# Retention products of the values as three rounded products, with split keys, weights and values, and rotation tables loaded by tile

## The chip, the core and the metric

One core of a Trainium2 chip. The metric is the device time of one execution in microseconds (us). The core has TensorE (PE in the profile; PEld is its weight load), VectorE (DVE), ScalarE (ACT), GpSimd (POOL) and SyncE (SP), which issues nearly all transfers. Each engine has its own queue and works it off in order; they wait for one another by semaphores.

## The reference

One layer of an encoder over 1024 frames of width 1024: a projection, a gated linear attention (GLA), a retention branch with rotary keys and queries, their mixture, and a convolutional feed-forward part. The change lies in the retention branch: 4 heads, key width 256, value width 512.

```python
def step(state, inp):
    qi, ki, vi = inp
    scores = jnp.einsum('bhnd,bhmd->bhnm', qi, ki) * intra_decay
    o = jnp.einsum('bhnm,bhme->bhne', scores, vi) + \
        jnp.einsum('bhnd,bhde->bhne', qi * q_decay, state)
    state = chunk_decay * state + jnp.einsum('bhmd,bhme->bhde', ki * k_decay, vi)
    return state, o
...
rq = rope(r_q.astype(f32).reshape(b, s, RET_HEADS, RET_DK), positions)
rk = rope(r_k.astype(f32).reshape(b, s, RET_HEADS, RET_DK), positions)
o_ret = retention_mixer(rq, rk, r_v.astype(f32))
o_ret = from_chunks(head_layernorm(o_ret)) * jax.nn.silu(r_g.astype(f32))
```

## The kernel before

The kernel runs in phases: normalisation, projection, GLA, retention, the output products of both branches, the mixture, the feed-forward up and down parts. Everything is written out engine by engine, with semaphore counts as the only link; nothing is scheduled automatically. Where precision is wanted, a float32 operand is split into a rounded part and a rest (`_hi`, `_lo`), and `product3` makes three products in a rounded type (fp32r) of them: hi times hi, hi times lo, lo times hi. The retention branch before makes plain float32 products.

The retention loop has RS = 32 steps e = 0 to 31, for 8 tiles of 128 frames (t = e // 4) and 4 heads (h = e % 4). "Weights times values" and "state inputs" are its two products with the values `r_v`:

- PE, step e: `key_transposes(e)` (2 transposes into KT_BANK; not in the last tile, e >= 28), `scores(e)`, for e < 28 one side piece (12 rounded products of a projection that has nothing to do with retention, L421 to L423), `out_transposes(e-2)`, `output(e-1)` (weights `r_pt` times values, and from the second tile on two products of the queries with the state), `state_inputs(e-1)` (two products of keys `r_kdt` with values; not for the last tile).
- ScalarE, step e: `keys(e)` reads KT_BANK and writes `r_kdt`, then `rstd(e-1)`, two small steps of the normalisation; in odd steps it empties a bank of the side work.
- VectorE, step e: `weights(e)` (scores times decay), `gate(e-2)`, `outputs(e-1)` (BN_STATS and BN_AGGR of PE's output, then, after `rstd`, the scaling `r_onb`), `states(e-1)`, two updates of the state. In the last tile `outputs(e-1)` comes ahead of `gate(e-2)`, and the outputs take turns in two banks (`out_bank`). In the last two steps the splitting of the next phase's operands follows (`mixed_lo`).
- GpSimd, step e: the rotation of queries and keys (two 128x512 products with `cossin`, two 128x256 sums, and the decayed queries `r_qdb`); in every fourth step it splits one slab of weights as well (`split_slab`). Its sums of step e wait for the output of step e-4. After the loop's last rotation it splits two slabs.
- SyncE, step e: loads of queries and keys four steps ahead, store of step e-2, gates, side store, values three steps ahead, and every fourth step a slab.

After the loop come `out_transposes(30)` and the first product of the next phase, `gated_half(0, 0)`, which needs the splits of ScalarE and VectorE.

## Time and profile before

| | |
|---|---|
| median of 3 runs (lowest to highest) | 2283.79 us (2283.73 to 2285.35) |
| the profiled execution, its own time | 2283.65 us |
| its span, first to last instruction | 2281.9 us |
| mean granted TensorE clock | 0.997 |
| busy: PE, DVE, ACT, POOL | 2247.3, 1209.6, 665.5, 1547.6 us |

The span is the time between the first and the last instruction of the program; the device time has 1.75 us around it. PE's busy time is the union of its records, whose ends are modelled: distances between the starts of records tell more than their lengths. A plain float32 matmul shows as two records, a rounded one as one.

### The profile page before, as it was taken

To read this page: it belongs to the slowest core of one execution; us is meant where nothing else is said; L and a number is where in the kernel's file an instruction comes from. 1 tells how busy PE (TensorE), PEld (TensorE's weight loads), DVE (VectorE), ACT (ScalarE), POOL (GpSimd) and SP (SyncE) were. 2 spreads that over 40 slices of the span, in tenths; PEclk is the share of its full clock that TensorE was granted. 3 is DMA by queue.
4 is the path that set the end of the run, shared out by engine and by line. 5 is a ranking of instruction groups with operands and counts; after the bars stand their busy time and mean duration, and the time that the engine had idled before them with its cause. 6 is when DMAs were issued, how large, how long until landed. Compare 5 with 4: busy or idle time off the path is not lost. (4 is left out here: it accounts for less than half of the span.)

```text
span 2281.9 us, 27553 instructions
## 1 busy us (share of the span) xinstructions
PE 2247.3 (98%) x10462; PEld 1834.1 (80%) x10462; DVE 1209.6 (53%) x1271; ACT 665.5 (29%) x1021; POOL 1547.6 (68%) x954
## 2 busy tenths in 40 slices
PE   8999999999999999999999999999999999999998
PEld 7888888899888888876665888878778888888887
DVE  6322222222728887844446444223867777776564
ACT  4323333221222222211113211114444444443422
POOL 5787777766446555578664468871999999964442
PEclk9999999999999999999999999999999999999999
DMA  4333333322362333265556556642222222345444
GB/s 178 102 111 111 111 111 111 111 93 100 120 232 91 106 112 117 92 209 167 161 166 210 192 207 213 225 171 107 78 74 84 84 84 83 93 158 209 144 139 152
DMA packets 174717, 309.06 MB, mean 135 GB/s; under 512 B 12225, under 2 KB 90305, under 8 KB 174593
## 3 DMA queue, kind: packets, MB, share of 16 engines
q1 hardware_dynamic: 174160, 306.27, 40.7%
q8 instruction: 81, 1.33, 0.2%
q10 hardware_dynamic: 432, 1.11, 0.1%
q14 instruction: 44, 0.35, 0.0%
HBM read 217.16 MB, written 90.18 MB: 135 GB/s over the span
## 5 line engine op out<-in xcount | busy, mean ns | idle before, releaser
L421 PE MATMUL psum<-act_hi,w_hi 128*128 128x512 f32 x1272 | 506.0, 398 | 2.6 <-POOL w_lo L3063 1.2
L423 PE MATMUL psum<-act_hi,w_lo 128*128 128x512 f32 x1272 | 497.4, 391 | 0.0
L422 PE MATMUL psum<-act_lo,w_hi 128*128 128x512 f32 x1272 | 496.4, 390 | 0.0
L421 PEld LDWEIGHTS psum<-act_hi,w_hi 128*128 128x128 f32 x1272 | 239.7, 188 | 51.1 <-POOL w_lo L3063 2.5
L423 PEld LDWEIGHTS psum<-act_hi,w_lo 128*128 128x128 f32 x1272 | 239.3, 188 | 51.6
L422 PEld LDWEIGHTS psum<-act_lo,w_hi 128*128 128x128 f32 x1272 | 239.8, 189 | 47.2
L455 POOL TENSOR_TENSOR w_hi<-w_raw,zero_col 128x1024 fp32r<-128x1024 f32 x53 | 109.2, 2060 | 167.1 <-PE psum L423 149.4
L3105 POOL TENSOR_TENSOR w_lo<-w_raw,w_hi 128x1024 fp32r<-128x1024 f32 x44 | 110.8, 2522 | 126.2 <-ACT w_hi L3116 126.2
L1530 POOL TENSOR_TENSOR k_lev<-e_t,g_x 128x896 f32<-128x896 f32 x32 | 96.3, 3011 | 127.5 <-ACT e_t L1477 92.3
L1062 POOL TENSOR_TENSOR w_lo<-w_raw,w_hi 128x512 fp32r<-128x512 f32 x80 | 105.0, 1313 | 65.0 <-ACT w_hi L1020 65.0
L2793 DVE TENSOR_TENSOR d_lob<-d_raw,d_hib 128x512 fp32r<-128x512 f32 x44 | 102.2, 2327 | 86.6 <-ACT d_hib L2787 86.6
L458 POOL TENSOR_TENSOR w_lo<-w_raw,w_hi 128x1024 fp32r<-128x1024 f32 x53 | 143.8, 2713 | 4.2
L421 PE MATMUL psum<-w_hi,act_hi 128*128 128x512 f32 (+1 forms) x384 | 139.7, 364 | 1.7 <-POOL w_lo L458 1.5
L423 PE MATMUL psum<-w_hi,act_lo 128*128 128x512 f32 (+1 forms) x384 | 139.3, 363 | 0.0
L422 PE MATMUL psum<-w_lo,act_hi 128*128 128x512 f32 (+1 forms) x384 | 139.3, 363 | 0.0
L421 PE MATMUL psum<-w_hi,d_hib 128*128 128x512 f32 x352 | 137.3, 390 | 1.4 <-DVE act_f L2832 0.7
L422 PE MATMUL psum<-w_lo,d_hib 128*128 128x512 f32 x352 | 137.0, 389 | 0.0
L423 PE MATMUL psum<-w_hi,d_lob 128*128 128x512 f32 x352 | 137.0, 389 | 0.0
L3063 POOL TENSOR_TENSOR w_lo<-w_raw,w_hi 128x512 fp32r<-128x512 f32 x80 | 125.5, 1579 | 2.8 <-ACT w_hi L3131 2.8
L421 PE MATMUL psum<-a_sums,w_hi 128*128 128x512 f32 x320 | 124.5, 389 | 0.0
L422 PE MATMUL psum<-a_sums,w_hi 128*128 128x512 f32 x320 | 124.5, 389 | 0.0
L423 PE MATMUL psum<-a_sums,w_lo 128*128 128x512 f32 x320 | 124.5, 389 | 0.0
(300 smaller groups left out, 4957.7 us busy)
## 6 DMA issues: line engine op xcount, KB each, us to landing
w_raw<-in_w_stream SPq DMA_DIRECT2D x225, 512.0 KB, 4.0
proj_scratch<-stage SPq DMA_DIRECT2D x40, 512.0 KB, 5.2
r_x<-proj_scratch SPq DMA_DIRECT2D x64, 256.0 KB, 3.2
value_scratch<-stage SPq DMA_DIRECT2D x24, 512.0 KB, 3.6
proj_scratch<-side_out SPq DMA_DIRECT2D x48, 256.0 KB, 3.0
d_raw<-ffn_scratch SPq DMA_DIRECT2D x44, 256.0 KB, 3.6
ffn_scratch<-u_lin_v SPq DMA_DIRECT2D x20, 512.0 KB, 5.8
r_v<-value_scratch SPq DMA_DIRECT2D x32, 256.0 KB, 2.7
```

The lines of the kernel that those rows point to most:

```text
L421: nc.tensor.matmul(o, s_hi, m_hi, start=start, stop=False)
L422: nc.tensor.matmul(o, s_hi, m_lo, start=False, stop=False)
L423: return nc.tensor.matmul(o, s_lo, m_hi, start=False, stop=stop)
L455: nc.gpsimd.tensor_tensor(w_hi[:, j, :], w_raw[:, j, :], zero_col[:, :].to_broadcast((P, D)), ALU.add).then_inc(sem["hi_split"], 1)
L458: nc.gpsimd.tensor_tensor(w_lo[:, j, :], w_raw[:, j, :], w_hi[:, j, :].bitcast(F32), ALU.subtract).then_inc(sem["slab_ready"], 1)
L1062: nc.gpsimd.tensor_tensor(w_lo8[:, n % 8, :], row_block(p, i), w_hi8[:, n % 8, :].bitcast(F32), ALU.subtract).then_inc(sem["u_lo"], 1)
L1530: nc.gpsimd.tensor_tensor(k_lev[:, b, :, :], levels, key.unsqueeze(1).to_broadcast((P, NL, P)), ALU.mult).then_inc(sem["g_klev"], 1)
L2793: nc.vector.tensor_tensor(d_lob[:, slot, :], d_raw[:, slot, :], d_hib[:, slot, :].bitcast(F32), ALU.subtract).then_inc(sem["d_lo"], 1)
L3063: nc.gpsimd.tensor_tensor(w_lo8[:, n % 8, :], block_raw(p, i), w_hi8[:, n % 8, :].bitcast(F32), ALU.subtract).then_inc(sem["u_lo"], 1)
L3105: nc.gpsimd.tensor_tensor(w_lo[:, j, :], w_raw[:, j, :], w_hi[:, j, :].bitcast(F32), ALU.subtract).then_inc(sem["slab_ready"], 1)
```

## The change

The values are split into `r_v_hi` (ScalarE, `values_hi`) and `r_v_lo` (VectorE, in the place of `r_v`), the keys into `r_kdt` (now a rounded type) and `r_kdt_lo`, the weights into `r_pt_hi` and `r_pt_lo`. `output` and `state_inputs` call `product3`. ScalarE makes one copy more in each step, VectorE three or four instructions, PE waits for `r_lo`. The rotation tables `cossin` are kept for two tiles instead of all eight and come with the queries of head 0. At e = 28 four loads go ahead of the slab's load instead of behind it.

```diff
-            cossin = sb(s, "cossin", (P, 2, SEQ))
+            cossin = sb(s, "cossin", (P, 2, 2, P))
+        def values_hi_count(e):
+            return RS - HEADS + e + 1 if last_tile(e) else 2 * e + 2
...
+        def rope_tables(sp, t, landed):
+            sp.dma_start(cossin[:, t % 2, :, :], rope_d[:, :, tile_cols(t)].rearrange("a p n -> p a n")
+                         ).then_inc(landed, 16)
...
+                if h == 0:
+                    rope_tables(sp, t, r_in[h])
...
-                if e % 4 == 0:
-                    stream_load(sp, SL_SIDE + 23 + e // 4)
                 if e == MIXED_STEP - 2:
                     sp.wait_ge(sem["r_rope"], 2 * RS)
                     sp.wait_ge(sem["r_qd"], RS)
-                    for h in range(HEADS):
-                        sp.wait_ge(r_v_in[h], 32 + 16 * NT)
                     for i in range(4):
+                        sp.wait_ge(r_v_in[i], 32 + 16 * NT)
                         mixed_load(sp, i)
+                if e % 4 == 0:
+                    stream_load(sp, SL_SIDE + 23 + e // 4)
...
+            def values_hi(e):
+
+                h = e % HEADS
+                act.wait_ge(r_v_in[h], 32 + 16 * (e // HEADS) + 16)
+                if e >= 2:
+                    act.wait_ge(sem["r_u"], min(e - 1, RS - HEADS))
+                    act.wait_ge(sem["r_o"], e - 1)
+                nc.scalar.activation(r_v_hi[:, e % 2, :], r_v[:, h, :], ACT.Copy
+                                     ).then_inc(sem["r_kd"], 1)
...
+                values_hi(e)
...
-                nc.vector.tensor_tensor(r_pt[:, e % 2, :], psum[:, RS_BANK, 0:P], ret_dec[:, e % HEADS, :], ALU.mult
+                raw = r_pt[:, e % 2, :]
+                nc.vector.tensor_tensor(raw, psum[:, RS_BANK, 0:P], ret_dec[:, e % HEADS, :], ALU.mult
                                         ).then_inc(sem["r_P"], 1)
+                dve.wait_ge(sem["r_P"], 3 * e + 1)
+                nc.vector.tensor_copy(r_pt_hi[:, e % 2, :], raw).then_inc(sem["r_P"], 1)
+                dve.wait_ge(sem["r_P"], 3 * e + 2)
+                nc.vector.tensor_tensor(r_pt_lo[:, e % 2, :], raw, r_pt_hi[:, e % 2, :].bitcast(F32), ALU.subtract
+                                        ).then_inc(sem["r_P"], 1)
+
+            def low_parts(e):
+
+                h, b = e % HEADS, e % 2
+                if not last_tile(e):
+                    dve.wait_ge(sem["r_kd"], 2 * e + 1)
+                    if e >= 2:
+                        dve.wait_ge(sem["r_u"], e - 1)
+                    nc.vector.scalar_tensor_tensor(r_kdt_lo[:, b, :], psum[:, KT_BANK, 0:RET_DK], ret_k[:, h:h + 1],
+                                                   r_kdt[:, b, :].bitcast(F32), ALU.mult, ALU.subtract
+                                                   ).then_inc(sem["r_lo"], 1)
+                dve.wait_ge(sem["r_kd"], values_hi_count(e))
+                nc.vector.tensor_tensor(r_v_lo[:, h, :], r_v[:, h, :], r_v_hi[:, b, :].bitcast(F32),
+                                        ALU.subtract).then_inc(sem["r_lo"], 1)
...
+                if e < RS - 1:
+                    low_parts(e)
...
                 if e == RS - 2:
                     weights(RS - 1)
+                    low_parts(RS - 1)
...
             def key_transposes(e):
                 if e:
-                    pe.wait_ge(sem["r_kd"], e)
+                    pe.wait_ge(sem["r_kd"], 2 * e - 1)
+                    pe.wait_ge(sem["r_lo"], 2 * e - 1)
...
-                pe.wait_ge(sem["r_P"], e + 1)
+                pe.wait_ge(sem["r_P"], 3 * e + 3)
+                pe.wait_ge(sem["r_kd"], values_hi_count(e))
+                pe.wait_ge(sem["r_lo"], values_hi_count(e))
...
-                last = nc.tensor.matmul(o, r_pt[:, b, :], r_v[:, h, :], start=True, stop=e < HEADS)
+                last = product3(o, r_pt_hi[:, b, :], r_pt_lo[:, b, :], r_v_hi[:, b, :], r_v_lo[:, h, :], True, e < HEADS)
...
-                pe.wait_ge(sem["r_kd"], e + 1)
+                pe.wait_ge(sem["r_kd"], 2 * e + 2)
+                pe.wait_ge(sem["r_lo"], 2 * e + 2)
...
-                    last = nc.tensor.matmul(psum[:, U_BANK + a, :], r_kdt[:, e % 2, a * P:(a + 1) * P],
-                                            r_v[:, e % HEADS, :], start=True, stop=True)
+                    cols = slice(a * P, (a + 1) * P)
+                    last = product3(psum[:, U_BANK + a, :], r_kdt[:, e % 2, cols], r_kdt_lo[:, e % 2, cols],
+                                    r_v_hi[:, e % 2, :], r_v_lo[:, e % HEADS, :], True, True)
```

The diff leaves out the places of the new tiles, the renamed semaphore of the rotation angles, and the matching counts. In `low_parts(e)` the call comes on VectorE between `outputs(e-1)` (in the last tile `gate(e-2)`) and `states(e-1)`.

VectorE in step 9 of the loop, before, from the gating on (the names in brackets are the semaphores waited for):

```order
L1995 TENSOR_TENSOR r_ogb<-psum,r_x 128x512 [waits r_ogst1,r_onT,gate_in3]
L2004 BN_STATS r_bst<-psum 128x6 [waits r_o]
L2006 BN_AGGR r_mvb<-r_bst 128x2 [waits r_bn]
L2011 TENSOR_SCALAR r_onb<-psum,r_mvb,r_rsb 128x512 [waits r_onT,r_mv,r_rstd]
L2022 SCALAR_TENSOR_TENSOR r_st<-r_st,psum 128x512 [waits r_u]
L2022 SCALAR_TENSOR_TENSOR r_st<-r_st,psum 128x512
L1986 TENSOR_TENSOR r_pt<-psum,ret_dec 128x128 [waits r_o,r_S]
```

The same place with the change:

```order
L2042 TENSOR_TENSOR r_ogb<-psum,r_x 128x512 [waits r_ogst1,r_onT,gate_in3]
L2051 BN_STATS r_bst<-psum 128x6 [waits r_o]
L2053 BN_AGGR r_mvb<-r_bst 128x2 [waits r_bn]
L2058 TENSOR_SCALAR r_onb<-psum,r_mvb,r_rsb 128x512 [waits r_onT,r_mv,r_rstd]
L2029 SCALAR_TENSOR_TENSOR r_kdt_lo<-psum,ret_k,r_kdt 128x256 [waits r_u,r_kd]
L2033 TENSOR_TENSOR r_v_lo<-r_v,r_v_hi 128x512 [waits r_kd]
L2069 SCALAR_TENSOR_TENSOR r_st<-r_st,psum 128x512 [waits r_u]
L2069 SCALAR_TENSOR_TENSOR r_st<-r_st,psum 128x512
L2014 TENSOR_TENSOR r_pt<-psum,ret_dec 128x128 [waits r_o,r_S]
L2017 CAST r_pt_hi<-r_pt 128x128 [waits r_P]
L2019 TENSOR_TENSOR r_pt_lo<-r_pt,r_pt_hi 128x128 [waits r_P]
```

The two low parts stand between the scaling `r_onb` and the state updates, and the weights of the next step are three instructions.

PE in step 9, from output 8 to the key transposes of step 10, in the kernel before, where L2089 is the product with the state, L2099 the state inputs and L2059 the key transposes (this place and the next are the same step of the loop):

```order
L2086 MATMUL psum<-r_v,r_pt 128x512 [waits r_state,rows_in0,r_on,r_qd,r_P]
L2089 MATMUL psum<-r_st,r_qdb 128x512 x2
L2099 MATMUL psum<-r_v,r_kdt 128x512 [waits r_state,r_kd]
L2099 MATMUL psum<-r_v,r_kdt 128x512
L2059 MATMUL psum<-ident,r_qk 128x128 [waits r_kd,r_rope]
L2059 MATMUL psum<-ident,r_qk 128x128
```

With the change:

```order
L428 MATMUL psum<-r_v_hi,r_pt_hi 128x512 [waits r_qd,r_state,r_lo,r_on,r_kd,r_P]
L429 MATMUL psum<-r_v_lo,r_pt_hi 128x512
L430 MATMUL psum<-r_v_hi,r_pt_lo 128x512
L2141 MATMUL psum<-r_st,r_qdb 128x512 x2
L428 MATMUL psum<-r_v_hi,r_kdt 128x512 [waits r_state,r_lo,r_kd]
L429 MATMUL psum<-r_v_lo,r_kdt 128x512
L430 MATMUL psum<-r_v_hi,r_kdt_lo 128x512
L428 MATMUL psum<-r_v_hi,r_kdt 128x512
L429 MATMUL psum<-r_v_lo,r_kdt 128x512
L430 MATMUL psum<-r_v_hi,r_kdt_lo 128x512
L2110 MATMUL psum<-ident,r_qk 128x128 [waits r_lo,r_kd,r_rope]
L2110 MATMUL psum<-ident,r_qk 128x128
```

The transposes of the keys (L2110) now wait for `r_lo` too, and both products with the values are rows of L428 to L430.

VectorE in the last tile, around the scaling of output 28, before:

```order
L1986 TENSOR_TENSOR r_pt<-psum,ret_dec 128x128 [waits r_o,r_S]
L2004 BN_STATS r_bst<-psum 128x6 [waits r_o]
L2006 BN_AGGR r_mvb<-r_bst 128x2 [waits r_bn]
L2011 TENSOR_SCALAR r_onb<-psum,r_mvb,r_rsb 128x512 [waits r_onT,r_mv,r_rstd]
L1995 TENSOR_TENSOR r_ogb<-psum,r_x 128x512 [waits r_ogst1,r_onT,gate_in3]
L1986 TENSOR_TENSOR r_pt<-psum,ret_dec 128x128 [waits r_o,r_S]
```

With the change:

```order
L2019 TENSOR_TENSOR r_pt_lo<-r_pt,r_pt_hi 128x128 [waits r_P]
L2051 BN_STATS r_bst<-psum 128x6 [waits r_o]
L2053 BN_AGGR r_mvb<-r_bst 128x2 [waits r_bn]
L2058 TENSOR_SCALAR r_onb<-psum,r_mvb,r_rsb 128x512 [waits r_onT,r_mv,r_rstd]
L2042 TENSOR_TENSOR r_ogb<-psum,r_x 128x512 [waits r_ogst1,r_onT,gate_in3]
L2033 TENSOR_TENSOR r_v_lo<-r_v,r_v_hi 128x512 [waits r_kd]
L2014 TENSOR_TENSOR r_pt<-psum,ret_dec 128x128 [waits r_o,r_S]
L2017 CAST r_pt_hi<-r_pt 128x128 [waits r_P]
L2019 TENSOR_TENSOR r_pt_lo<-r_pt,r_pt_hi 128x128 [waits r_P]
L2051 BN_STATS r_bst<-psum 128x6 [waits r_o]
```

The low part of the values of step 29 stands behind the gating of step 27, which stands behind output 28.

## Rows read from the trace of the kernel before

**Rows 1.** The page's first part: busy us, share of the span, instructions.

```profile
PE 2247.3 (98%) x10462; PEld 1834.1 (80%) x10462; DVE 1209.6 (53%) x1271; ACT 665.5 (29%) x1021; POOL 1547.6 (68%) x954
```

**Rows 2.** Table of windows: length, busy us, PEclk, DMA share, GB/s.

```profile
1037.18:1208.68 171.50, 171.50 (x673) 108.39 (x672) 79.33 (x148) 25.38 (x74) 122.62 (x120) 1.00 0.54 161
```

**Rows 3.** Timeline of one step: start us, us, engine, line, operation, [idle before].

```profile
1102.51 0.38 PE L2059 MATMUL psum<-ident,r_qk 128*128 128x128 f32 x2
...
1105.26 0.39 PE L421 MATMUL psum<-act_hi,w_hi 128*128 128x512 f32 x1
...
1105.95 0.60 PE L2108 MATMUL psum<-ident,r_onb 128*128 128x128 f32 x4
...
1106.39 1.02 PE L2086 MATMUL psum<-r_v,r_pt 128*128 128x512 f32 x2
...
1108.96 1.88 PE L2099 MATMUL psum<-r_v,r_kdt 128*128 128x512 f32 x4
...
1109.16 0.70 DVE L2004 BATCH_NORM_STATS2 r_bst<-psum 128x6 f32<-128x512 f32 x1 [1.83 <-PE psum L2089]
...
1110.68 0.81 DVE L2011 TENSOR_SCALAR r_onb<-psum,r_mvb,r_rsb 128x512 f32<-128x512 f32 x1 [0.60 <-ACT r_rsb L1960]
1110.68 0.38 PE L2059 MATMUL psum<-ident,r_qk 128*128 128x128 f32 x2
...
1111.41 1.28 DVE L2022 SCALAR_TENSOR_TENSOR r_st<-r_st,psum 128x512 f32<-128x512 f32 x2
...
1112.60 0.29 DVE L1986 TENSOR_TENSOR r_pt<-psum,ret_dec 128x128 f32<-128x128 f32 x1
```

**Rows 4.** Instructions of lines 1587 and 2793: duration ns min/median/max.

```profile
L1587 DVE SCALAR_TENSOR_TENSOR g_st<-g_st,g_deccol,psum x24: 470/472/477, 749.7 to 963.0; 128x256 f32<-128x256 f32 x24
...
L2793 DVE TENSOR_TENSOR d_lob<-d_raw,d_hib x44: 680/2466/2894, 2029.5 to 2254.4; 128x512 fp32r<-128x512 f32 x44
```

**Rows 5.** Timeline of the last steps of the loop.

```profile
1216.85 0.81 DVE L2011 TENSOR_SCALAR r_onb<-psum,r_mvb,r_rsb 128x512 f32<-128x512 f32 x1 [0.60 <-ACT r_rsb L1960]
...
1217.71 0.66 PE L2108 MATMUL psum<-ident,r_onb 128*128 128x128 f32 x4 [0.26 <-DVE r_onb L2011]
...
1223.29 1.89 POOL L1365 TENSOR_TENSOR w_hi<-w_raw,zero_col 128x1024 fp32r<-128x1024 f32 x1
...
1223.46 1.10 PE L2086 MATMUL psum<-r_v,r_pt 128*128 128x512 f32 x2 [0.35 <-POOL r_qdb L1935]
...
1226.99 1.02 PE L2086 MATMUL psum<-r_v,r_pt 128*128 128x512 f32 x2
...
1230.45 1.02 PE L2086 MATMUL psum<-r_v,r_pt 128*128 128x512 f32 x2
...
1239.69 1.08 PE L2108 MATMUL psum<-ident,r_onb 128*128 128x128 f32 x4 [3.48 <-DVE r_ogb L1995]
```

**Rows 6.** Timeline in the down projection, GpSimd and VectorE.

```profile
2111.08 2.39 POOL L3105 TENSOR_TENSOR w_lo<-w_raw,w_hi 128x1024 fp32r<-128x1024 f32 x1 [3.05 <-ACT w_hi L3116]
...
2111.55 2.46 DVE L2793 TENSOR_TENSOR d_lob<-d_raw,d_hib 128x512 fp32r<-128x512 f32 x1 [2.98 <-ACT d_hib L2787]
```

**Rows 7.** Timeline of GpSimd in a step with a slab.

```profile
1101.13 0.72 POOL L1930 TENSOR_TENSOR r_qk<-r_xcb,r_xsb 128x256 f32<-128x256 f32 x1 [3.45 <-PE psum L2089]
...
1103.30 1.90 POOL L1365 TENSOR_TENSOR w_hi<-w_raw,zero_col 128x1024 fp32r<-128x1024 f32 x1
...
1105.28 2.36 POOL L1368 TENSOR_TENSOR w_lo<-w_raw,w_hi 128x1024 fp32r<-128x1024 f32 x1
```

**Rows 8.** Timeline of the loop's first steps, GpSimd and PE.

```profile
990.31 1.27 POOL L1921 TENSOR_TENSOR r_xcb<-r_x,cossin 128x512 f32<-128x512 f32 x1 [9.74 <-DMA cossin<-rope_scratch]
...
1003.65 0.44 PE L2059 MATMUL psum<-ident,r_qk 128*128 128x128 f32 x2 [1.08 <-POOL r_qk L1932]
```

**Rows 9.** Table of windows: stretches with PE idle in or ahead of them.

```profile
1637.00:1643.00 6.00, 4.29 (x19) 3.19 (x19) 4.99 (x5) 1.61 (x2) 6.00 (x3) 1.00 0.47 164
1240.00:1246.00 6.00, 6.00 (x18) 4.84 (x17) 5.37 (x11) 3.56 (x8) 0.00 (x0) 0.55 0.92 274
```

More of the change, by code:

```diff
@@ L189 @@
 small_in wd_zero wd_hi lr_hi lr_out z_out z_copied z_abs z_exp z_ln log_a loga_stored
-pos_f turns0 turns1 angle angle_red sin_half cos_sq rope_done rope_stored
+turns0 turns1 angle angle_red sin_half cos_sq rope_done rope_stored
 proj_evac val_half val_evac st0 st1 st2 st3
@@ L194 @@
 side_evac side_st0 side_st1 side_st2
-r_tab_in r_in0 r_in1 r_in2 r_in3 gate_in0 gate_in1 gate_in2 gate_in3 r_xc r_xs r_rope r_qd r_kT r_kd r_S r_P r_o r_u r_state
+r_tab_in r_in0 r_in1 r_in2 r_in3 gate_in0 gate_in1 gate_in2 gate_in3 r_xc r_xs r_rope r_qd r_kT r_kd r_S r_P r_o r_u r_lo r_state
 r_bn r_mv r_lnv r_rstd r_on r_onT r_og r_ogst0 r_ogst1 a_hi a_lo y_sig
@@ L292, in build @@
             r_st = sb(s, "r_st", (P, HEADS, 2, RET_DV))
-            r_kdt = sb(s, "r_kdt", (P, 2, RET_DK))
-            r_pt = sb(s, "r_pt", (P, 2, P))
+            r_kdt = sb(s, "r_kdt", (P, 2, RET_DK), F32R)
+            with ExitStack() as s2:
+                r_pt = sb(s2, "r_pt", (P, 2, P))
+            r_pt_lo = sb(s, "r_pt_lo", (P, 2, P), F32R)
             r_onb = sb(s, "r_onb", (P, 2, RET_DV))
@@ L299, in build @@
             r_rsb = sb(s, "r_rsb", (P, 2, 2))
-            r_pad = sb(s, "r_pad", (P, 288))
+            r_pt_hi = sb(s, "r_pt_hi", (P, 2, P), F32R)
+            r_pad = sb(s, "r_pad", (P, 32))
             r_x = sb(s, "r_x", (P, HEADS, 8, P))
-            r_v = sb(s, "r_v", (P, HEADS, RET_DV))
-            cossin = sb(s, "cossin", (P, 2, SEQ))
+            with ExitStack() as s2:
+                r_v = sb(s2, "r_v", (P, HEADS, RET_DV))
+            r_v_lo = sb(s, "r_v_lo", (P, HEADS, RET_DV), F32R)
+            cossin = sb(s, "cossin", (P, 2, 2, P))
+            r_v_hi = sb(s, "r_v_hi", (P, 2, RET_DV), F32R)
+            r_kdt_lo = sb(s, "r_kdt_lo", (P, 2, RET_DK), F32R)
             ret_dec = sb(s, "ret_dec", (P, HEADS, P))
@@ L752, in proj_dve @@
             log_a_tail(NT - 1)
-            nc.vector.tensor_copy(ang[:, 1, :], pos_i[:, :]).then_inc(sem["pos_f"], 1)
-            dve.wait_ge(sem["pos_f"], 1)
+            nc.vector.tensor_copy(ang[:, 1, :], pos_i[:, :]).then_inc(sem["angle"], 1)
+            dve.wait_ge(sem["angle"], 1)
             nc.vector.tensor_scalar(ang[:, 0, :], ang[:, 1, :], invf[:, 0:1], None, ALU.mult
                                     ).then_inc(sem["angle"], 1)
-            dve.wait_ge(sem["angle"], 1)
+            dve.wait_ge(sem["angle"], 2)
             magic = 1.5 * 2.0 ** 23
@@ L768, in proj_dve @@
                                                ALU.mult, ALU.add).then_inc(sem["angle"], 1)
-                dve.wait_ge(sem["angle"], i + 2)
+                dve.wait_ge(sem["angle"], i + 3)
             nc.vector.tensor_scalar(ang[:, 0, :], ang[:, 0, :], 3.1415925, -3.1415925,
@@ L1856, in ret_early_loads @@
             sp.wait_ge(sem["g_dec"], NT * HEADS)
-            sp.dma_start(cossin[:, :, :], rope_d.rearrange("a p n -> p a n")).then_inc(sem["r_tab_in"], 16)
+            rope_tables(sp, 0, sem["r_tab_in"])
         def ret_first_loads(sp):
@@ L1915, in ret_pool @@
                 x4 = r_x[:, h, 0:4, :]
-                pool.wait_ge(r_in[h], 16 * t + 16)
-                cos = cossin[:, 0, tile_cols(t)].unsqueeze(1).to_broadcast((P, 4, P))
-                sin = cossin[:, 1, tile_cols(t)].unsqueeze(1).to_broadcast((P, 4, P))
+                pool.wait_ge(r_in[h], 16 * t + 16 + (16 * t if h == 0 else 0))
+                cos = cossin[:, t % 2, 0, :].unsqueeze(1).to_broadcast((P, 4, P))
+                sin = cossin[:, t % 2, 1, :].unsqueeze(1).to_broadcast((P, 4, P))
                 if e >= 2:
@@ L1949, in keys @@
                     act.wait_ge(sem["r_u"], e - 1)
+                    act.wait_ge(sem["r_lo"], 2 * e - 3)
                 nc.scalar.activation(r_kdt[:, e % 2, :], psum[:, KT_BANK, 0:RET_DK], ACT.Copy,
@@ L2065, in scores @@
                 if e:
-                    pe.wait_ge(sem["r_P"], e)
+                    pe.wait_ge(sem["r_P"], 3 * e - 2)
                 for a in range(2):
@@ L2074, in output @@
                 o = psum[:, out_bank(e), :]
-                pe.wait_ge(sem["r_P"], e + 1)
+                pe.wait_ge(sem["r_P"], 3 * e + 3)
+                pe.wait_ge(sem["r_kd"], values_hi_count(e))
+                pe.wait_ge(sem["r_lo"], values_hi_count(e))
                 pe.wait_ge(sem["r_qd"], e + 1)
-                pe.wait_ge(r_v_in[h], 32 + 16 * (e // HEADS) + 16)
                 if e >= HEADS:
```

## The prediction

> **What bounds the kernel now.** The page comes first: PE is busy for 2247.3 of 2281.9 us and every other engine far less [rows 1], so a change is worth what it does to TensorE's queue: work taken out of it, and waits put into it. The second view is the table of windows over the stretch that the change touches. The stretch runs from the key transposes of step 6 to those of step 27 of the retention loop, 21 steps. PE is busy for 171.50 of 171.50 us at a granted clock of 1.00, VectorE for 79.33, ScalarE for 25.38, GpSimd for 122.62 [rows 2]. Here PE sets the pace with no wait at all. The third view is the timeline of one step [rows 3]. PE goes through key transposes (1102.51), scores, a side piece, output transposes, output (1106.39), state inputs (1108.96) and the next key transposes (1110.68): 8.17 us, and the stretch agrees, 171.50 / 21 = 8.17.
>
> **Products: a saving.** A plain float32 product is two records: the state inputs, two products, last from 1108.96 to 1110.68, so 0.86 us each. Three rounded products of the same shape run from 1105.26 to 1105.95, 0.69 us [rows 3]. The change converts one product in each of 32 outputs and two in each of 28 state inputs, 88 in all. PE's own work falls by 88 x 0.17 = 15.0 us, by 0.17 in an output and 0.34 in a state input. Its work in a full step becomes 8.17 - 0.51 = 7.66 us.
>
> **One wait that did not exist.** The transposes of step e+1 overwrite the bank KT_BANK. Before, they waited only for ScalarE's `keys(e)`, done early in step e. Now VectorE reads that bank too, for `r_kdt_lo` of step e, and the transposes wait for it (`r_lo`). The order shows where that instruction stands on VectorE: behind `outputs(e-1)`, hence behind PE's `output(e-1)`, which is the last thing but one that PE does before those transposes. So PE may not pass from step e to e+1 until the normalisation of the output it has just made is finished. What is queued behind the wait is everything PE has.
>
> Worked out from one step [rows 3], with the statistics' start as zero. BN_STATS starts at 1109.16 and the scaling `r_onb` at 1110.68: 1.52 us, with ScalarE's two small steps inside. The next VectorE instruction starts 0.73 later (1111.41): 2.25. Then comes `r_kdt_lo`, 128x256 from PSUM with a pointer scalar and an SBUF operand. Line 1587 is that very form and takes 0.47 (470 to 477 ns) [rows 4]: 2.72. From VectorE's end to PE's start I take 0.1: in the tail `r_onb` ends at 1217.66 and PE starts at 1217.71, an operand from VectorE, 0.05, and the first record of such a wait is 0.06 longer (0.66 against 0.60) [rows 3, 5]. I round the two to 0.16, so the transposes effectively start at 2.88. Before they started at 1.52. The state inputs that cover this wait end at 1.52 - 0.34 = 1.18, so PE stands for 1.7 us in each step.
>
> The output itself ends 0.17 earlier, so a step grows by 2.88 - 1.52 - 0.17 = 1.19 us, from 8.17 to 9.36. Steps 1 to 4 have no state product in their output, but the same chain and the same two conversions. Transposes 2 to 27 wait in this way, 26 of them: 26 x 1.19 = **+30.9 us**. The last output before the tail gives -0.2. Bounds: `r_kdt_lo` at least 0.28 (`r_pt`, 128x128, whose row ends the step) and at most 0.68 (a half of the pair at 1111.41, 128x512), and 0.05 to 0.2 for the signal: 1.0 to 1.5 a step, +26 to +39.
>
> **The other new VectorE work.** Per step these are `r_v_lo` (128x512, about 0.69), the rounding of the weights and their rest (128x128, at most 0.28 each when free). They come behind `r_kdt_lo`, and the product that needs them starts 3.88 us after the transposes (1102.51 to 1106.39). Free-running, they are hidden. They have two SBUF operands, though, and such an instruction stood still in the trace: `d_lob`, issued 0.47 us into a GpSimd subtraction, took 2.46 and ended 0.54 after it; its shortest was 0.68 [rows 4, 6]. In a step without a slab GpSimd starts on the rotation when the output ends and has no work from about 4.8 us on, since it waited 3.45 us for the next output [rows 7]. `r_v_lo` then ends at 4.2, the state updates at 5.4, the weights' parts at 6.2, and the next statistics are wanted at 9.36. In one of the seven steps with a slab (two more instructions, 1.90 and 2.36) the same chain ends near 8.9. Cost 0, with about 0.5 us of cover; the upper bound is a whole further GpSimd operation, 2.4 us, in seven steps.
>
> The Trainium skill ("SBUF — State Buffer", Who interferes with whom) says that a VectorE instruction with two SBUF inputs, or a copy in a two-port mode, and a GpSimd instruction that reads SBUF exclude each other for the whole instruction, and whichever issues first has the port. This trace agrees for two inputs (2.46 against 0.68 us); no copy of this form is in it. By the rule the rounding of the weights would also stand behind GpSimd, which is the second rival below.
>
> **ScalarE, SyncE and the tables.** `values_hi`, 32 copies, falls in ScalarE's idle time (25.38 busy of 171.50). The rotation tables come as eight parts and not as one transfer. GpSimd's first rotation waited 9.74 us for that transfer [rows 8], and PE then waited 1.08 for the keys of step 1. A part an eighth as long should land earlier by more than that: **-1.1 us**, between 0 and -1.1. The remaining parts are loaded a tile ahead.
>
> **The tail.** From step 28 there are no key transposes, but `r_v_lo` of step e now stands behind `outputs(e-1)` and, past step 28, behind a gating as well. The two output banks therefore no longer overlap. Before, outputs started at 1223.46, 1226.99 and 1230.45 [rows 5]. Now one follows the other by 2.25 (statistics to the end of scaling), 0.69 (gating), 0.69 (`r_v_lo`), 0.1, then 0.69 + 1.71 + 0.2 for the output until its statistics: 6.3 us. Two such distances cost 5.7, and the delay of the two outputs ahead of them (`r_v_lo` of 27 and 28) about 2. Some 2 come back, because the last output was followed by a 3.48 us wait for splits that now come together: 5.5. GpSimd splits two slabs in just this stretch, from 1223.29 on, and can hold up three of these VectorE instructions by up to 2.4 us each. PE idles long enough for its clock to drop: after 3.48 us without work the granted clock was 0.55, near the 1.2 GHz level, for 6 us [rows 5, 9]. I take **+8 us**, between +4 and +12.
>
> **The sum**, against the profiled execution's own 2283.65 us, 0.14 below the median of the three runs: 2283.65 - 1.1 + 30.9 - 0.2 + 8 = 2321.3, so **2321 us**. Nothing later absorbs it: PE is full again in the stage that follows, and GpSimd there waits for PE.
>
> **The rivals.**
> *The wait is covered (faster).* If `r_kdt_lo` were finished before the state inputs, only the saving would stay: 2283.65 - 15.0 - 1.1 = 2267.5. It decides at 1.69 us from the start of the statistics to the transposes (1.52 + 0.17), or 1.4 with the tail counted. Against it: the chain has used 1.52 before `r_onb` even begins. For it: only that the order could be read wrongly. 0.04.
> *GpSimd locks VectorE out.* If rounding, rest and `r_v_lo` each lose a GpSimd operation, VectorE reaches the next statistics late, by 1 to 4 us in the seven slab steps: 2328 to 2350, about 2338. For it speaks the standstill in [rows 6], against it the 4 us for which GpSimd has nothing to do in the other steps. 0.10.
> *The clock drops in the loop.* PE would now idle 1.7 us in 9.4. At 1.2 GHz 7.66 us of work takes about 15.3, and 26 steps come to some +180: 2500 us. Against it: the stretch 1637 to 1643, with PE at work for 4.29 of 6 us, kept a clock of 1.00 [rows 9]. 0.04.
> *Nothing changes.* Gains and waits would have to cancel. 0.02.
> The forecast has the remaining 0.80.
>
> **From these to the numbers.** The forecast's own terms span 2283.65 + 26 + 4 - 1.1 = 2312.6 to 2283.65 + 39 + 12 = 2334.7. The range 2309 to 2337 adds to it the lower half of the second rival. A run differs from no change when it is off by 0.2%, 4.6 us: faster 0.04, same 0.02, slower 0.94.
>
> **What would show it.** In the profile of the changed kernel: PE idle about 1.7 us before each key transpose and this put down to VectorE's `r_kdt_lo`; steps of 9.36 us; `r_kdt_lo` of 0.47 us starting 2.25 after the statistics; three rounded records in 0.69 us; PE's total busy time lower by some 10 to 15 us though the span is longer; output starts in the tail some 6 us apart; no wait of 1.08 us in step 1. The prediction is wrong if the transposes follow the state inputs with no gap, if the step's gap is ended by another instruction, or if the granted clock in the loop is under 1.00.

## The result, and the profile after

The changed kernel takes 2329.24 us (median of 4 runs, 2325.76 to 2330.3) against 2283.76 for the kernel before on the same chip (2282.87 to 2285.35): a ratio of 1.0195, interval 1.0182 to 1.0208. It is slower by 45 us, 2%. The profiled execution took 2329.68 us, its span is 2327.9.

The page's first part, in the form of [rows 1], shows PE with 4.2 us less work in a span that is 46 us longer; its share falls from 98 to 96%:

```profile
PE 2243.1 (96%) x10550; PEld 1850.7 (80%) x10550; DVE 1306.1 (56%) x1395; ACT 682.0 (29%) x1053; POOL 1560.3 (67%) x954
```

The table of windows (length, then busy us of PE, its weight load, VectorE, ScalarE and GpSimd, then granted clock, DMA share and GB/s) has the same 21 steps as [rows 2], from the transposes of step 6 to those of step 27 (first row). The two rows behind it are used further down: a stretch in the early steps and one in the tail.

```profile
1045.52:1242.23 196.71, 164.88 (x735) 118.35 (x736) 140.21 (x232) 36.20 (x94) 127.56 (x116) 1.00 0.49 144
1026.90:1032.00 5.10, 5.07 (x19) 4.11 (x20) 4.43 (x6) 0.99 (x2) 4.89 (x5) 0.67 0.44 137
1269.50:1274.00 4.50, 4.48 (x8) 2.38 (x9) 0.53 (x3) 0.00 (x0) 0.00 (x0) 0.56 0.17 51
```

A step now takes 196.71 / 21 = 9.37 us instead of 8.17. PE's busy time fell from 171.50 to 164.88 us while the stretch grew by 25.2, so PE stands for 31.8 us in it, 1.52 per step. The list of waits of PE from 1000 to 1290 names what ends them (us in total, times, longest):

```profile
PE psum L2110 <- DVE r_kdt_lo L2029: 38.5, 25, 2.1
PE psum L428 <- DVE r_pt L2014: 8.4, 2, 5.5
PE psum L2110 <- POOL r_qk L1945: 2.3, 1, 2.3
```

And the timeline of one step has the whole chain, to be laid beside [rows 3]:

```profile
1126.97 0.70 DVE L2051 BATCH_NORM_STATS2 r_bst<-psum 128x6 f32<-128x512 f32 x1 [0.36 <-PE psum L2141]
...
1127.69 0.39 PE L429 MATMUL psum<-r_v_lo,r_kdt 128*128 128x512 f32 x1
...
1127.92 0.39 PE L430 MATMUL psum<-r_v_hi,r_kdt_lo 128*128 128x512 f32 x1
...
1128.48 0.81 DVE L2058 TENSOR_SCALAR r_onb<-psum,r_mvb,r_rsb 128x512 f32<-128x512 f32 x1 [0.60 <-ACT r_rsb L1986]
1129.21 0.47 DVE L2029 SCALAR_TENSOR_TENSOR r_kdt_lo<-psum,ret_k,r_kdt 128x256 fp32r<-128x256 f32 x1
1129.45 1.27 POOL L1936 TENSOR_TENSOR r_xcb<-r_x,cossin 128x512 f32<-128x512 f32 x1
1129.60 1.67 DVE L2033 TENSOR_TENSOR r_v_lo<-r_v,r_v_hi 128x512 fp32r<-128x512 f32 x1
...
1129.83 0.41 PE L2110 MATMUL psum<-ident,r_qk 128*128 128x128 f32 x2 [1.52 <-DVE r_kdt_lo L2029]
...
1136.33 0.70 DVE L2051 BATCH_NORM_STATS2 r_bst<-psum 128x6 f32<-128x512 f32 x1 [1.67 <-PE psum L2141]
```

With the statistics' start as zero, the scaling starts at 1.51, the keys' low part at 2.24 and the transposes at 2.86. The next statistics start at 9.36. Seen from VectorE, the keys' low part is short and never late in itself: it is simply queued behind the scaling.

The same rows hold a second thing. The values' low part was issued 0.15 us after a GpSimd product and took 1.67 us. Its shortest record in this run is 0.68, and its 22 records in the 21 steps have a mean of 1.69. So GpSimd holds VectorE up by about 1 us in every full step. PE does not wait for it there: what ends its wait, the keys' low part, starts earlier and takes 0.47 us.

The tail, from the transposes of step 27 on, holds the other large loss. PE waits 5.50 and 2.88 us for the weights of a step. On the way to the first of these waits, two small VectorE instructions ran beside GpSimd's slabs and took 2.45 and 1.97 us (their shortest records are 0.29 and 0.68):

```profile
1259.68 2.34 POOL L1372 TENSOR_TENSOR w_hi<-w_raw,zero_col 128x1024 fp32r<-128x1024 f32 x1
...
1262.10 2.34 POOL L1375 TENSOR_TENSOR w_lo<-w_raw,w_hi 128x1024 fp32r<-128x1024 f32 x1
1262.14 2.45 DVE L2019 TENSOR_TENSOR r_pt_lo<-r_pt,r_pt_hi 128x128 fp32r<-128x128 f32 x1
...
1266.42 2.34 POOL L465 TENSOR_TENSOR w_lo<-w_raw,w_hi 128x1024 fp32r<-128x1024 f32 x1
...
1267.34 1.97 DVE L2033 TENSOR_TENSOR r_v_lo<-r_v,r_v_hi 128x512 fp32r<-128x512 f32 x1
...
1269.52 0.76 PE L428 MATMUL psum<-r_v_hi,r_pt_hi 128*128 128x512 f32 x1 [5.50 <-DVE r_pt L2014]
...
1277.83 0.47 PE L428 MATMUL psum<-r_v_hi,r_pt_hi 128*128 128x512 f32 x1 [2.88 <-DVE r_pt L2014]
```

Where the 46.0 us between the two profiled executions lie can be read from two starts. The transposes of step 6 start at 1045.52 against 1037.18: 8.3 us up to there. Those of step 27 start at 1242.23 against 1208.68, 33.6 us, so the 21 full steps cost 25.2. The rest, 12.5 us, comes behind them.

### The profile page after: what moved, and what is told of

Read it like the earlier page. It is cut to its first block and busy times, and to the rows that moved or that the text cites. A ratio compares the mean times of both kernels' runs of the same rounds, so it can differ in the third digit from the quotient of the medians.

```text
span 2327.9 us, 27974 instructions
## 1 busy us (share of the span) xinstructions
PE 2243.1 (96%) x10550; PEld 1850.7 (80%) x10550; DVE 1306.1 (56%) x1395; ACT 682.0 (29%) x1053; POOL 1560.3 (67%) x954
## 5 line engine op out<-in xcount | busy, mean ns | idle before, releaser
L428 PE MATMUL psum<-act_hi,w_hi 128*128 128x512 f32 x1272 | 506.3, 398 | 4.8 <-DVE act_lo L2233 2.2
L430 PE MATMUL psum<-act_hi,w_lo 128*128 128x512 f32 x1272 | 497.7, 391 | 0.0
L428 PEld LDWEIGHTS psum<-act_hi,w_hi 128*128 128x128 f32 x1272 | 239.7, 188 | 54.0 <-DVE act_lo L2233 2.6
L430 PEld LDWEIGHTS psum<-act_hi,w_lo 128*128 128x128 f32 x1272 | 239.6, 188 | 51.6
L428 PE MATMUL psum<-w_hi,act_hi 128*128 128x512 f32 (+1 forms) x384 | 139.7, 364 | 1.8 <-POOL w_lo L465 1.5
L430 PE MATMUL psum<-w_hi,act_lo 128*128 128x512 f32 (+1 forms) x384 | 139.3, 363 | 0.0
L428 PE MATMUL psum<-w_hi,d_hib 128*128 128x512 f32 x352 | 137.3, 390 | 1.4 <-DVE act_f L2886 0.7
L430 PE MATMUL psum<-w_hi,d_lob 128*128 128x512 f32 x352 | 137.0, 389 | 0.0
L428 PE MATMUL psum<-a_sums,w_hi 128*128 128x512 f32 x320 | 124.5, 389 | 0.0
L430 PE MATMUL psum<-a_sums,w_lo 128*128 128x512 f32 x320 | 124.5, 389 | 0.0
```

What stands on the lines that cost most here:

```text
L428: nc.tensor.matmul(o, s_hi, m_hi, start=start, stop=False)
L430: return nc.tensor.matmul(o, s_lo, m_hi, start=False, stop=stop)
```

## The experiments

Eleven further kernels ran. The theory on trial is that of **place**: what costs the time is where the low parts stand on VectorE, behind the scaling of the output. The first rival is the **port**: VectorE's new instructions with two SBUF operands are held by GpSimd. A second question came up on the way, the **clock**.

**1. The keys' low part alone, moved ahead of the statistics.**

```diff
                 if e < RS - 1:
                     weights(e)
+                    low_keys(e)
...
                 if e < RS - 1:
-                    low_parts(e)
+                    low_values(e)
```

> The changed kernel, with VectorE's low part of the keys put right behind weights(e) instead of behind outputs(e-1); nothing else differs. Place theory (the loss is PE's wait for an instruction that stands behind the normalisation): the 1.5 us gap before each key transpose goes, a full step falls from 9.37 to about 7.7 us, and what stays is the saving of 15 us, the start's 1 us and the longer tail of some 12: 2280 us (2276 to 2287). Port theory (the loss is VectorE and GpSimd excluding each other, new with the splits on VectorE): the same instructions still collide, 2310 us or more.

Measured: 2282.82 us, ratio 0.9996 (0.9986 to 1.0005). One instruction of 0.47 us, moved by some lines, takes back 46 us. The same 21 steps:

```profile
1037.68:1199.25 161.57, 161.56 (x736) 119.80 (x735) 139.34 (x234) 35.15 (x96) 134.50 (x123) 1.00 0.60 177
```

In these steps PE has no wait left and a step is 7.69 us. VectorE carries the same new work as in the changed kernel and is busy as long (139.34 against 140.21 us): GpSimd still holds it up, now mostly in the splits of the weights (means of 0.83 and 0.96 us), and this costs the loop nothing. That speaks against the port as the cause of the loop's cost; the next experiment settles it, because its one new instruction is never held up.

**2. The wait alone, in the kernel before.** The keys' low part is computed at its late place into a tile that nobody reads, PE waits for it, and the products stay as they were.

```diff
+                if not last_tile(e):
+                    low_keys(e)
                 if e:
...
                     pe.wait_ge(sem["r_kd"], e)
+                    pe.wait_ge(sem["r_lo"], e)
```

> The kernel before with one thing of the change alone: the key low part's instruction in its place behind outputs(e-1), written to a tile that nobody reads, and PE's wait for it before the next key transposes. All products stay plain float32, nothing else is split. Place theory: each of 26 steps grows by 2.88 - 1.52 = 1.36 us, with the tail as before: 2283.8 + 35.4 = 2319 us (2316 to 2322), steps of 9.53 us. Port theory: this instruction has PSUM as its other operand and does not collide, so about 2284 us.

Measured: 2318.8 us, ratio 1.0152 (1.0135 to 1.0169). The list of waits of PE:

```profile
PE psum L2073 <- DVE r_junk L2021: 30.8, 26, 1.2
```

The instruction took 0.47 to 0.48 us in all its 28 records, and nothing else is new on VectorE. A step takes 9.52 us, 1.35 more than before. That is 2.88 - 1.52, the chain's growth as forecast, without the 0.17 that the output's products give back. Behind step 27 nothing changes (1073.4 us to the end of the span, 1073.2 before).

**3. Both low parts moved ahead.**

```diff
                     weights(e)
+                    low_parts(e)
...
-                if e < RS - 1:
-                    low_parts(e)
```

> The changed kernel with the whole of low_parts(e), keys and values, put behind weights(e). Place theory: as in the run before, and the tail's outputs no longer wait for the normalisation of the output before them, so the 12 us of the tail go too: 2268 us (2264 to 2276), below the kernel before. If the values' low part, now ahead of the statistics, is held up by GpSimd, it delays the statistics by up to 1.5 us a step, which no longer stands between PE and its next work. Port theory: 2310 us or more.

Measured: 2277.9 us, ratio 0.9977 (0.9967 to 0.9986): a real gain over the kernel before, 10 us short of what I expected. The loop gives all of it, 10.2 us in 21 steps (161.29 against 171.50, 7.68 us a step). What is missing lies around it (in the profiled execution, whose 2280.61 us are above the median). Ahead of the transposes of step 5 PE waits 2.11 us for GpSimd's rotation, and the 9.30 us behind them have a granted clock of 0.82, so that the transposes of step 6 start no earlier than before (1037.57). And behind step 27 the run takes 6.8 us more than before. The timeline shows why; GpSimd, VectorE and PE:

```profile
1215.21 2.35 POOL L1375 TENSOR_TENSOR w_lo<-w_raw,w_hi 128x1024 fp32r<-128x1024 f32 x1
1215.46 2.18 DVE L2017 CAST r_pt_hi<-r_pt 128x128 fp32r<-128x128 f32 x1
1217.52 1.89 POOL L462 TENSOR_TENSOR w_hi<-w_raw,zero_col 128x1024 fp32r<-128x1024 f32 x1
1217.68 1.88 DVE L2019 TENSOR_TENSOR r_pt_lo<-r_pt,r_pt_hi 128x128 fp32r<-128x128 f32 x1
...
1220.37 0.77 PE L428 MATMUL psum<-r_v_hi,r_pt_hi 128*128 128x512 f32 x1 [2.66 <-DVE r_pt_lo L2019]
```

Each of the two small VectorE instructions ends just after the GpSimd instruction beside it.

**4. Both ahead in the last tile only**, the loop left as changed (`low_parts(e)` behind `weights(e)` where `last_tile(e)`).

> The changed kernel with low_parts(e) put behind weights(e) in the last tile alone (steps 28 to 31). Place theory: the loop's steps stay at 9.37 us and only the tail shortens, by 9 to 12 us: 2318 us (2316 to 2322). Port theory: GpSimd's two slabs run there either way and hold the same instructions up, so at most 3 us are gained: 2326 or more.

Measured: 2322.56 us, ratio 1.0175 (1.0158 to 1.0192). Behind step 27 the profiled execution now takes 7.2 us more than before instead of 12.5: by this pair the place explains 5.3 us of the tail, less than expected; some 1.9 us of the gain lie ahead of step 6, where the two kernels are the same. The 7.2 us that stay are close to the 6.8 of experiment 3, and the timeline has the same picture: `r_pt_lo` takes 2.46 us and `r_v_lo` 2.38, beside GpSimd's two slabs.

Experiment 1 is a caution against taking the 5.3 us as exact. The values' low part stands in its late place there too, and still its profiled execution has only 6.4 us more behind step 27 than before, no more than experiment 3 with that part moved ahead, although by the medians experiment 3 is the faster by 4.9 us. The timed executions of one kernel differ by some microseconds (2280.06 to 2285.81 in experiment 1), and how the two engines meet in the tail may also depend on the loop ahead of it; no run separates the two.

**5. GpSimd's last slabs held back** (experiment 3, with this; SyncE's load behind the held slab moves to the end of its list).

```diff
+            pool.wait_ge(sem["r_lo"], 2 * RS - HEADS)
             split_slab(pool, SL_SIDE + 26)
```

> The kernel with both low parts behind the weights, 2277.9 us, and GpSimd's last two slabs held back until the last low part of the values is written, so that GpSimd is idle while VectorE splits the last tile's weights; SyncE's load behind the held slab is moved to the end of its list. Theory (the missing 10 us of that run lie partly in the tail, where the cast took 2.18 us and the low part of the weights 1.88 us beside GpSimd's slabs, against 0.23 and 0.29 us without): both fall under 0.3 us, output (29)'s wait of 2.66 us shrinks to under 0.5, the clock stays at 1.00 behind it, and the run takes 2274.5 us (2272 to 2276.5). Rival (those long instructions are not GpSimd's doing, or the wait is hidden by another): 2277 to 2280 us.

Measured: 2281.58 us, ratio 0.9988 (0.998 to 0.9997); expected 2274.5, a miss, with the reason visible. (One of its twelve executions took 4907.88 us at a granted clock of 1.00, and no cause is known; without it the median is 2281.54.) VectorE's splits are freed, and the slabs then hold what VectorE does next:

```profile
1213.92 0.23 DVE L2019 CAST r_pt_hi<-r_pt 128x128 fp32r<-128x128 f32 x1
1214.18 0.29 DVE L2021 TENSOR_TENSOR r_pt_lo<-r_pt,r_pt_hi 128x128 fp32r<-128x128 f32 x1
...
1224.26 8.03 DVE L2234 TENSOR_TENSOR act_lo<-a_raw,act_hi 128x512 fp32r<-128x512 f32 x4
1224.42 2.27 POOL L1372 TENSOR_TENSOR w_hi<-w_raw,zero_col 128x1024 fp32r<-128x1024 f32 x1 [12.66 <-DVE r_v_lo L2035]
...
1235.04 2.48 DVE L2234 TENSOR_TENSOR act_lo<-a_raw,act_hi 128x512 fp32r<-128x512 f32 x4
1235.27 1.09 PE L2163 MATMUL psum<-ident,r_onb 128*128 128x128 f32 x4 [7.97 <-DVE r_ogb L2044]
```

The rounding takes 0.23 us here against 2.18 in experiment 3, and four low parts of the mixed inputs take 8.03 us beside the slabs against 2.48 eleven microseconds later without them. The holding-up is GpSimd's doing, both ways round, and moving it only chooses the victim: the wait of 2.66 us went, and the next wait for a gating grew from 2.44 to 7.97.

**6. Experiment 5, with the order of the tail changed** on ScalarE (the last values' high part first) and VectorE (the mixed inputs' low parts behind the next statistics and gating).

> The same with two changes of order in the tail: ScalarE writes the last head's values' high part ahead of the four high parts of the mixed inputs, and VectorE does the statistics of output (30) and the gate of (29) ahead of the first four low parts of the mixed inputs. Expected: the wait of output (31) of 1.41 us goes and the wait of 2.44 us for the gate falls to about 1 us; 2271.5 us (2268.5 to 2275). Rival: the mixed inputs' low parts are then late for the next products, and nothing or little is gained: 2274 to 2277 us.

Measured: 2282.24 us, ratio 0.9995 (0.9986 to 1.0003): no better than experiment 5. The rival's reason holds, though its 2274 to 2277 us, reckoned from the 2274.5 that experiment 5 was to take, do not. The mixed inputs are late; the wait of 7.97 us comes back as six of 1.3 to 2.0 us between 1228 and 1252.

**7. Two products in the state inputs instead of three**, in the changed kernel.

```diff
-                    last = product3(psum[:, U_BANK + a, :], r_kdt[:, e % 2, cols], r_kdt_lo[:, e % 2, cols],
-                                    r_v_hi[:, e % 2, :], r_v_lo[:, e % HEADS, :], True, True)
+                    nc.tensor.matmul(psum[:, U_BANK + a, :], r_kdt[:, e % 2, cols], r_v_hi[:, e % 2, :],
+                                     start=True, stop=False)
+                    last = nc.tensor.matmul(psum[:, U_BANK + a, :], r_kdt[:, e % 2, cols], r_v_lo[:, e % HEADS, :],
+                                            start=False, stop=True)
```

> The changed kernel with only two of the three rounded products in the state inputs (keys' low part times values' high part is left out of the computation; its instruction on VectorE stays, and so does the wait for it). This takes 2 products of 0.23 us out of each of 28 steps, 12.9 us of TensorE work. Theory (the step is set by the chain from the statistics over the normalized output to the keys' low part, which starts when the output's products end, ahead of the state inputs): the state inputs end 0.46 us sooner and the wait of the transposes grows from 1.52 to 1.98 us; no gain, 2329 us (2325 to 2332). Rival (TensorE's own work sets the loop, or VectorE waits for the state inputs): the whole gain, 2316 us (2313 to 2320).

This leaves one product out of the computation and serves the timing alone. Measured: 2348.51 us, ratio 1.0284 (1.0269 to 1.0299). 12.9 us of work were taken out of PE, and the kernel became 19.3 us *slower* than the changed one. Neither theory had that. The wait is what the place theory says, 1.97 us per step (1.52 + 0.46). The windows of two steps in a row, from transposes to transposes, show the rest; both hold the same 34 products, and the clock is the third number from the end:

```profile
1045.93:1056.89 10.96, 8.99 (x34) 6.53 (x34) 8.39 (x12) 1.49 (x4) 9.25 (x8) 0.84 0.35 106
1056.89:1066.27 9.38, 7.40 (x34) 5.26 (x34) 6.11 (x12) 1.98 (x5) 5.08 (x6) 1.00 0.44 130
```

One step runs at a granted clock of 1.00 and takes 9.38 us, as in the changed kernel: the products taken out were covered. The other is granted 0.84 on average and takes 10.96. In it a part of the products start 0.42 us apart, near the 1.2 GHz level, and the later ones 0.23 us apart:

```profile
1048.28 0.63 PE L428 MATMUL psum<-act_hi,w_hi 128*128 128x512 f32 x1
1048.70 0.63 PE L429 MATMUL psum<-act_lo,w_hi 128*128 128x512 f32 x1
...
1050.06 0.39 PE L430 MATMUL psum<-act_hi,w_lo 128*128 128x512 f32 x1
1050.29 0.39 PE L428 MATMUL psum<-act_hi,w_hi 128*128 128x512 f32 x1
```

Twelve of the 21 steps are of the long kind: 12 x 1.6 = 19 us, the whole loss.

**8. The keys' low part done twice**, the first time into a tile that nobody reads, to lengthen the wait with PE's work as it is.

```diff
+                    nc.vector.scalar_tensor_tensor(r_junk[:, :], psum[:, KT_BANK, 0:RET_DK], ret_k[:, h:h + 1],
+                                                   r_kdt[:, b, :].bitcast(F32), ALU.mult, ALU.subtract
+                                                   )
                     nc.vector.scalar_tensor_tensor(r_kdt_lo[:, b, :], psum[:, KT_BANK, 0:RET_DK], ret_k[:, h:h + 1],
```

> The changed kernel with the keys' low part written twice, first to a tile that nobody reads: 0.47 us more in the chain ahead of the transposes (2.86 us becomes 3.3), nothing more on TensorE. The steps' wait of 1.52 us grows to about 1.98 us, the length at which the run with two products lost its clock in two steps of three. Theory of the chain alone (it sets the step, microsecond for microsecond, and the clock stays at 1.00): 28 x 0.47 = 13 us more, 2342 us (2339 to 2345). Theory that a wait of this length also costs the clock, as it did there (steps of 9.37 and 10.97 us in place of 9.37): 2355 to 2372 us, with steps of two lengths some 1.5 us apart, and the granted clock of the longer ones below 0.95.

Measured: 2350.54 us, ratio 1.0286 (1.0271 to 1.0302), between the two expectations. The wait is 1.91 us (the second instruction starts 0.39 after the first, not 0.47), and again steps of two lengths:

```profile
1059.45:1069.20 9.75, 7.85 (x35) 5.64 (x36) 6.10 (x13) 1.98 (x5) 5.07 (x6) 1.00 0.43 121
1069.20:1080.58 11.38, 9.47 (x36) 6.97 (x36) 6.13 (x13) 1.49 (x4) 5.09 (x6) 0.85 0.43 127
```

Six of 21 are long. 21 x 0.39 for the chain and 6 x 1.6 for the clock make 17.8 us, and the stretch grew by 214.46 - 196.70 = 17.8. The mechanism is that of the second expectation, and the long steps are fewer. So a wait of 1.52 us per step keeps the clock, and waits of 1.91 and 1.97 lose it in some steps, whether TensorE's work is shorter or VectorE's chain longer.

**9. Two products, with both low parts ahead** (experiment 3 with the edit of experiment 7).

> The kernel with both low parts behind the weights, 2277.9 us in its timed runs, with the same two products of 0.23 us per step left out of the state inputs (keys' low part times values' high part is left out of the computation). Theory: where nothing waits for the low part, the loop is TensorE's own work, and 28 x 0.46 = 12.9 us come off: 2265 us (2262 to 2269). Rival (something else holds the step near 7.7 us, the statistics chain or GpSimd's rotations): 2274 to 2279 us.

Measured: 2271.67 us, ratio 0.9948 (0.9934 to 0.9963): 6.2 us less than experiment 3, not 12.9, and so between the two expectations. Without the wait the products do count: an undisturbed step takes 7.19 us instead of 7.68.

```profile
1052.30:1059.50 7.20, 7.20 (x35) 5.35 (x34) 6.16 (x13) 1.87 (x5) 6.91 (x8) 1.00 0.56 170
```

But GpSimd is busy for 6.91 of these 7.20 us. Where PE catches up with it, it waits: 3.39 us from 1024.56 on for the rotation of a step, and the transposes of step 6 start no earlier (1037.85). In the full steps PE has only two waits, 0.41 and 0.43 us, both for VectorE in a stretch with a slab. That GpSimd is the next bound of the loop is likely, and not shown: no run takes work off it.

**10. GpSimd's slabs spread anew**, with both low parts ahead. SyncE's loads move with the slabs, and ScalarE has the order of experiment 6, for which the expectation counts 0.7 us; the cut shows GpSimd's part alone.

```diff
+        SLABS_BEHIND = (0, 6, 10, 14, 18, 22, 25, 28)
...
-                if e % 4 == 0 and e < RS - HEADS:
-                    split_slab(pool, SL_SIDE + 19 + e // 4)
-            split_slab(pool, SL_SIDE + 26)
+                if e in SLABS_BEHIND:
+                    split_slab(pool, SL_SIDE + 19 + SLABS_BEHIND.index(e))
```

> Both low parts behind the weights (2277.9 us), with GpSimd's slabs placed anew: behind the rotations of steps 0, 6, 10, 14, 18, 22, 25 and 28, in place of 0, 4, 8 to 24 and the end (SyncE's loads moved with them), and the last head's values' high part ahead of the mixed inputs' on ScalarE. Expected: the rotation of step 5 is ready 4.5 us sooner, its wait of 2.11 us and the lower clock behind it go (-3.5 us); in the tail one slab stands in VectorE's way in place of two (the low part of the weights 0.3 in place of 1.88 us, output (29)'s wait of 2.66 us falls to about 1): -3 us; the order on ScalarE -0.7. 2271 us (2267 to 2275). Rival (these waits only move on to the mixed inputs and their loads, as when the slabs were held back): 2276 to 2281 us.

Measured: 2276.0 us, ratio 0.9966 (0.9952 to 0.9979): outside the 2267 to 2275 us expected, at the edge of the rival's 2276 to 2281, and the lowest median here of a kernel that computes everything. The tail behind step 27 is 2.6 us longer than before instead of 6.8. The early steps gained 1.5 of the 3.5 us expected (step 27 starts at 1197.37 instead of 1198.86): the wait for the rotation is gone, but one step of 9.5 us stays, in which PE waits 0.43 and 0.99 us for VectorE, and the one behind it takes 8.3. Against experiment 3 it gains 5.7 us between the profiled executions and 1.9 between the medians, so the size of this gain is not settled (runs of 2274.71 to 2277.2 against 2276.19 to 2281.71).

**11. The rotation tables by tile, alone, in the kernel before** (the tables' part of the diff of the change).

> The kernel before with the rotation tables loaded tile by tile and nothing else. Expected by my term for them: GpSimd's first rotation starts 1.2 us sooner (its idle time of 9.74 us falls to about 8.4), the wait of the second transposes (1.08 us) goes, and the run takes 2282.8 us (2281.5 to 2284.5), a gain at the edge of what can be timed: the trace decides. Rival (the six 128 KB loads between the heads' loads delay them, and GpSimd waits for its inputs): over 2285 us.

Measured: 2282.79 us, ratio 0.9993 (0.9984 to 1.0003), no difference that the timed runs can tell. The timeline has it: GpSimd's first rotation,

```profile
989.48 1.29 POOL L1928 TENSOR_TENSOR r_xcb<-r_x,cossin 128x512 f32<-128x512 f32 x1 [8.48 <-DMA cossin<-rope_scratch]
```

waited 8.48 us instead of 9.74 [rows 8]. The wait of 1.08 us ahead of the second transposes is not in the list any more, and the transposes of step 27 start at 1207.84 instead of 1208.68: 0.8 us gained, of the 1.1 in my sum.

## Why the prediction came out right, and what it missed

**The wait.** Predicted: transposes 2.88 us after the statistics, a step of 9.36, 30.9 us in 26 steps. Measured: 2.86, 9.37, and 1.20 us for each of the 21 full steps. Experiments 1 and 2 show that this wait is what costs the loop its time: taken away, the kernel is as fast as before; put alone into the kernel before, it costs 35 us. The signal to PE, rounded to 0.16, was 0.15. The forecast had PE standing for 1.7 us and the list has 1.52. The difference lies in how the records end: the last product ahead of the wait starts at 1127.92 with a record of 0.39 us, while in the queue the next one starts 0.23 after it (1127.69, 1127.92). From 1128.15 to the transposes at 1129.83 it is 1.68.

**The products.** A third of a microsecond per step in the state inputs counts for nothing while the wait stands behind them, as the prediction had it: in experiment 7 the undisturbed steps are as long as with three products. Without the wait, the loop shortens by 0.49 us a step (experiment 3), and the three conversions at 0.17 had made 0.51. PE's total fell by 4.2 us, though, not by the 10 to 15 I named as a sign. In the 21 full steps, all at a granted clock of 1.00, it fell by 6.6 us where 21 x 0.51 = 10.7 were converted, mostly for the reason just given: each wait adds the 0.16 us by which the last record outlasts its place in the queue. And the work in the tail and in one early stretch ran at a lower clock (0.56 and 0.67 in the windows above), which made it longer.

**VectorE's other work** was put at 0, with 0.5 us of cover in a slab step. The step that ends in the first statistics of the timeline above is one with a slab, and it has 0.36 us between the end of VectorE's work and those statistics. In the early steps the term was mis-sized. Those from 2 to 4 are shorter in PE's work, 6.4 us in the kernel before; with 1.19 each I forecast 7.6, and they took 8.26, 8.42 and 9.23. Three rows tell why:

```profile
1018.51 0.41 PE L2110 MATMUL psum<-ident,r_qk 128*128 128x128 f32 x2 [2.14 <-DVE r_kdt_lo L2029]
...
1021.05 2.50 DVE L2019 TENSOR_TENSOR r_pt_lo<-r_pt,r_pt_hi 128x128 fp32r<-128x128 f32 x1
...
1026.93 0.41 PE L2110 MATMUL psum<-ident,r_qk 128*128 128x128 f32 x2 [2.26 <-POOL r_qk L1945]
```

VectorE was held in both steps (the low parts of values and weights took 1.62 and 1.27 us in the first, that of the weights 2.50 in the second), the statistics came late, and PE waited 2.14 and 2.26 us. The list puts the second wait down to a rotation, which ended at 1026.79; the keys' low part ended at 1026.78, so it was both. Behind this wait the granted clock was 0.67 (second row of the windows above), and the third step took 9.23. Up to step 6 the sum had 4.9 us and the run has 8.3. Two of my signs of being wrong, a gap ended by another instruction and a clock under 1.00 in the loop, thus came true in this one early step; in the 21 full steps neither did.

**The tail** was put at +8, between 4 and 12, and is +12.5. The causes that I named were at work: outputs 28, 29 and 30 start at 1260.48, 1269.52 and 1277.83, 9.0 and 8.3 us apart (forecast 6.3, before 3.5). Of the 12.5 us the place makes about 5.3 by experiment 4, with the caution said there. The rest goes with GpSimd's slabs beside VectorE's splits (experiments 3, 5 and 10) and with the clock at 0.56 behind the wait of 5.50; how it divides is not shown. I had priced slabs and clock inside the 8, too low. With both terms at their measured size, 3.5 and 4.7 us more, 2321.3 becomes 2329.5; the profiled execution took 2329.68.

**The rivals.** The wait is covered only when the instruction is moved. The measured 2329 us lie inside the range of the second rival too (2328 to 2350), so the time alone does not choose between it and the forecast; the steps do. GpSimd locks VectorE out in every full step (mean of 1.69 us for `r_v_lo`) and most in those with a slab, and yet all 21 steps take 9.36 to 9.38 us, with a slab or without: the loss stays covered there. Outside the full steps it is not. The Trainium skill ("SBUF — State Buffer", Who interferes with whom) also lets a copy in a two-port mode be excluded. The trace agrees as far as it goes: the rounding `r_pt_hi` took 0.23 us free and 2.18 beside a slab (experiments 5 and 3). In what mode the copy ran no row shows. The keys' low part, with one of its operands in PSUM, stayed between 474 and 479 ns in its 28 records. The clock rival was given 4 in 100 and did not come true at a wait of 1.52 us in 9.37. I argued against it with a single stretch that had kept its clock; experiments 7 and 8 show that it was 0.4 us of waiting away. That part of the forecast came out right by a small margin, not by its argument.

What stays open: which of the waits of 1.9 us loses the clock and which does not, and how the remaining 2.6 us of the tail in experiment 10 divide between GpSimd, the order on ScalarE and the loads of the mixed inputs.

## What to carry to other kernels

Where the busiest engine reuses a buffer, look at who reads it last in program order, not only at how long that reader takes: half a microsecond of VectorE in each step, behind the wrong instruction, cost 46 us, and ahead of it nothing. Read a split of operands twice, once for the products it saves and once for the queue in which its low parts stand, and put these where their inputs are ready, ahead of work that still waits for a later result. Holding GpSimd off one pair of VectorE instructions is no gain unless the time in which it then runs is free of others.
